# TensorE's expert code as one looped body over 32 half experts, instead of 16 experts written out

## The reference

```
def expert_choice_ffn(h, w_router, w1, w3, w2):
    B, L, D = h.shape
    cap = EC_CAPACITY * L // N_EXPERTS
    aff = jax.nn.softmax((h @ w_router).astype(jnp.float32), axis=-1)
    gate, idx = lax.top_k(aff.transpose(0, 2, 1), cap)
    xs = jax.vmap(lambda hb, ib: hb[ib])(h, idx)
    a = jnp.einsum('becd,edf->becf', xs, w1)
    b = jnp.einsum('becd,edf->becf', xs, w3)
    y = jnp.einsum('becf,efd->becd', jax.nn.silu(a) * b, w2) * gate[..., None].astype(h.dtype)
    return jax.vmap(lambda yb, ib: jnp.zeros((L, D), yb.dtype).at[ib.reshape(-1)].add(yb.reshape(-1, D)))(y, idx)
```

## Time and profile before

| what | us |
|---|---|
| median of three runs | 3301.26 |
| the profiled execution, its own time | 3291.43 |
| its span (first to last instruction) | 3289.7 |
| first expert stage, about 1006 to 1612 | 606 |
| second expert stage, about 2638 to 3236 | 598 |
| TensorE busy in the span | 2851.3 |
| VectorE / ScalarE / GpSimd busy | 867.7 / 492.3 / 238.1 |

### The profile page before, as it was taken

One profiled execution on the slowest core, in us unless ns is written; L12 is line 12 of the kernel. 1 busy time (PEld: TensorE's weight loads), 2 busy tenths in 40 slices (PEclk: granted clock), 3 DMA queues, 4 the chain that ended last, 5 costly groups with the idle time before them and its releaser, 6 DMA issues.

```text
span 3289.7 us, 70042 instructions
## 1 busy us (share of the span) xinstructions
PE 2851.3 (87%) x32580; PEld 2092.8 (64%) x32580; DVE 867.7 (26%) x1443; ACT 492.3 (15%) x862; POOL 238.1 (7%) x254
## 2 busy tenths in 40 slices
PE   6999999999976887887579999999999678878874
PEld 3555676666646787877535456666666378777773
DVE  4953223231142000000159422223311400000003
ACT  2011023331020000000020110333200200000001
POOL 0330000000000000000004100000000000000000
PEclk9999999999988999999889999999999899999997
DMA  7222201102127999999762221121021289999994
GB/s 303 102 109 103 116 29 60 78 26 83 77 81 251 353 349 346 358 349 344 279 236 103 108 99 69 34 79 54 26 109 52 83 306 361 349 348 363 356 340 158
DMA packets 128912, 611.22 MB, mean 186 GB/s; under 512 B 6256, under 2 KB 6256, under 8 KB 119024
## 3 DMA queue, kind: packets, MB, share of 16 engines
q1 hardware_dynamic: 112464, 550.52, 44.1%
q0 software_dynamic: 7168, 24.12, 3.1%
q10 hardware_dynamic: 8992, 32.11, 2.6%
HBM read 576.84 MB, written 29.88 MB: 184 GB/s over the span
## 4 chain that ended last, share of the span: by engine, by line
PE 76%; issue 8%; DVE 8%; DMA 6%; ACT 1%; POOL 0%; POOLq 0%; SPq 0%; DVEq 0%; ACTq 0%
PE ps L281 65%; DVE region_b L1033 4%; DMA ring<-in_w_exp 3%; PE ps L524 2%; DMA ring<-in_w_mix 2%; PE ps L651 1%; PE ps L497 1%; PE ps L507 1%; PE ps L578 1%; PE ps L561 1%; DVE rstd L990 1%; DMA region_x<-ffn_rows 0%; DMA ffn_rows<-region_b,rstd 0%; DVE rstd L982 0%; PE ps L436 0%
## 5 line engine op out<-in xcount | busy, mean ns | idle before, releaser
L281 PE MATMUL ps<-region_r,ring 128*64 128x80 f32 x24192 | 927.6, 237 | 211.7 <-issue 200.3
L281 PEld LDWEIGHTS ps<-region_r,ring 128*64 128x64 f32 x24192 | 892.7, 140 | 248.8 <-issue 237.5
L281 PE MATMUL ps<-hT,ring 128*128 128x320 f32 (+2 forms) x3600 | 1019.2, 441 | 20.7 <-DVE region_b L1021 11.1
L281 PEld LDWEIGHTS ps<-hT,ring 128*128 128x128 f32 x3600 | 610.6, 192 | 380.3 <-issue 237.7
L281 PE MATMUL ps<-region_b,ring 128*128 128x320 f32 (+2 forms) x896 | 257.5, 439 | 3.6 <-DMA ring<-in_w_mix 3.6
L1033 DVE SCALAR_TENSOR_TENSOR region_b<-region_b,params 128x655 f32<-128x655 f32 x240 | 243.8, 1016 | 8.5
L1219 DVE TENSOR_TENSOR region_r<-ps,region_r 128x320 f32<-128x320 f32 x64 | 31.5, 492 | 741.4 <-PE ps L682 741.4
L281 PEld LDWEIGHTS ps<-region_b,ring 128*128 128x128 f32 x896 | 159.3, 191 | 75.8 <-issue 23.3
L954 ACT ACTIVATE region_r<-ps 128x320 f32<-128x320 f32 x64 | 28.0, 438 | 1067.1 <-PE ps L682 1067.1
L281 PE MATMUL ps<-region_x,ring 128*128 128x512 f32 (+1 forms) x480 | 137.7, 445 | 3.7 <-DVE region_x L1159 3.7
L1224 DVE COPY region_r<-ps 128x320 f32<-128x320 f32 x64 | 31.5, 492 | 364.8 <-PE ps L682 364.8
(11 more groups left out here) (193 smaller groups left out, 2009.8 us busy)
## 6 DMA issues: line engine op xcount, KB each, us to landing
ring<-in_w_exp SPq DMA_DIRECT2D x192, 2048.0 KB, 10.7
ring<-in_w_mix SPq DMA_DIRECT2D x68, 2048.0 KB, 11.4
x_store<-region_m ACTq DMA_DIRECT2D x2, 2560.0 KB, 12.1
ffn_rows<-region_r ACTq DMA_DIRECT2D x4, 1280.0 KB, 18.0
region_m<-x_store ACTq DMA_DIRECT2D x2, 2560.0 KB, 10.5
h_rows<-region_x ACTq DMA_DIRECT2D x10, 512.0 KB, 2.7
region_x<-ffn_rows ACTq DMA_DIRECT2D x4, 1280.0 KB, 9.4
rstd<-in_bias POOLq DMA_DIRECT2D x16, 192.0 KB, 2.7
```

The source lines that it names most:

```text
L281: ins = pe.matmul(*args, **kw)
```

## The change

TensorE's work is cut into 32 halves of experts. Half i = 2e + h of expert e has the w1 block and the w3 block of half h of its inner width, and then one w2 block: half h of the outputs of the expert before, e - 1. So each half is three blocks, and the halves look alike. Halves 0 to 2 stand in straight code (the first two without a w2 block), halves 3 to 31 are one body in a loop of TensorE (`pe.Fori(3, HALVES)`), and the two w2 blocks of the last expert follow in straight code. Semaphore values are worked out from the loop's counter in registers.

To make the halves alike, the rest follows: the rows come in halves of 512 columns (34 gathers of 80 x 2 KB, `xs_half`, with row numbers `slot_half` made by VectorE; the last two have no use), each turned between the w1 and the w3 block; VectorE parks them in `xs_next` and copies them to `xs` after the last w3 block of the expert; silu goes into one of two buffers `sil`, since `act` is still read by the w2 blocks; y is handled per half (`turn_y`, `scale_y`, `copy_y`). Products, shapes and weights stay the same. VectorE, ScalarE and GpSimd keep written-out code. The expert weights lie in HBM in the new order (`w_first`, `w_exp`, `w_last`), and SyncE's loop runs over 30 groups of three blocks.

The diff, cut to the parts that move work:

```diff
-                with sp.Fori(0, EPAIRS) as q:
-                    for b in range(2 * EXP_BLOCKS):
-                        s = (MIX_BLOCKS + b) % SLOTS
...
+                for b in range(FIRST_BLOCKS):
+                    expert_load(b, a["w_first"][l, b])
+                with sp.Fori(0, LOOP_BLOCKS // 3) as t:
+                    for b in range(3):
+                        expert_load(FIRST_BLOCKS + b, a["w_exp"][l, t, b], t)
+                for b in range(LAST_BLOCKS):
+                    expert_load(FIRST_BLOCKS + LOOP_BLOCKS + b, a["w_last"][l, b])
...
+                def expert_half(i, n, turns, second, y_before):
+
+                    pe.wait_ge(S["xs_ready"], i + 1 if type(i) is not int or i else 2)
+                    if type(i) is not int or i:
+                        pe.wait_ge(S["sil_ready"], i)
+                    expert_block(n, turns, a_ps, xs, "a_done")
+                    if type(i) is not int or i:
+                        pe.wait_ge(S["xs_parked"], i)
+                    turn_rows(i + 2, i + 3)
+                    if type(i) is not int or i:
+                        pe.wait_ge(S["b_used"], i)
+                    expert_block(n + 1, turns, b_ps, xs, "b_done")
+                    if y_before:
+                        turn_y(i - 3)
+                    if second:
+                        pe.wait_ge(S["act_ready"], i - 1)
+                        expert_block(n + 2, turns, y_ps, act, "y_done")
...
-                turn_rows(0)
-                for q in range(EPAIRS):
-                    expert_pair(q, q == 0, q == EPAIRS - 1)
-                turn_y(NE - 1)
+                turn_rows(0, 2, 0)
+                turn_rows(1, 2, 1)
+                expert_half(0, 0, 0, False, False)
+                expert_half(1, 2, 0, False, False)
+                expert_half(2, FIRST_BLOCKS, 0, True, False)
+                with pe.Fori(3, HALVES) as i:
+                    expert_half(i, FIRST_BLOCKS, i - 2, True, True)
+                for b in range(LAST_BLOCKS):
+                    turn_y(HALVES - 3 + b)
+                    pe.wait_ge(S["act_ready"], HALVES)
+                    expert_block(FIRST_BLOCKS + LOOP_BLOCKS + b, 0, y_ps, act, "y_done")
+                turn_y(HALVES - 1)
...
+                for i in range(HALVES):
+                    sc.wait_ge(S["a_done"], i + 1)
+                    if i >= 2:
+                        sc.wait_ge(S["act_ready"], i // 2 * 2)
+                    sc.activation(sil[i % 2], PS[0][:, 0, 0:HC], ACT.Silu).then_inc(S["sil_ready"], 1)
+                    if i >= 3:
+                        scale_y(i - 3)
...
+                for i in range(HALVES):
+                    e, half = divmod(i, 2)
+                    v.wait_ge(S["rows_turned"], i + 3)
+                    v.tensor_copy(xs_next[:, half * HC:(half + 1) * HC], PS[2][:, 0, 0:HC]).then_inc(S["xs_parked"], 1)
+                    v.wait_ge(S["b_done"], i + 1)
+                    v.wait_ge(S["sil_ready"], i + 1)
+                    if half == 0:
+                        v.tensor_tensor(sil[0], PS[0][:, 1, 0:HC], sil[0], ALU.mult).then_inc(S["b_used"], 1)
+                        if e:
+                            copy_y(i - 2)
+                        continue
                     if e < NE - 1:
-                        take_rows(e + 1)
...
+                        v.wait_ge(S["xs_parked"], i + 1)
+                        v.tensor_copy(flat(xs), xs_next).then_inc(S["xs_ready"], 2)
+                    if e:
+                        copy_y(i - 2)
+                    link(v.tensor_tensor(flat(act)[:, HC:2 * HC], PS[0][:, 1, 0:HC], sil[1], ALU.mult), "b_used")
+                    v.tensor_copy(flat(act)[:, 0:HC], sil[0]).then_inc(S["act_ready"], 2)
...
-                fetch_rows(0)
-                for e in range(NE):
-                    if e + 1 < NE:
-                        fetch_rows(e + 1)
-                    if e:
-                        add_rows(e - 1)
-                add_rows(NE - 1)
+                for n in range(3):
+                    fetch_rows(n)
+                for i in range(HALVES):
+                    if i + 3 < FETCHES:
+                        fetch_rows(i + 3)
+                    if i >= 4 and i % 2 == 0:
+                        add_rows((i - 4) // 2)
+                for e in range(NE - 2, NE):
+                    add_rows(e)
```

More of the change, by code:

```diff
@@ L43 @@
 CAP = CAPL + CAPC
-EPAIRS = NE // 2
+HALVES = 2 * NE
 EPS = 1e-6
@@ L71 @@
 EXP_BLOCKS = 6
+FIRST_BLOCKS, LOOP_BLOCKS, LAST_BLOCKS = 4, 3 * (HALVES - 2), 2
+FETCHES = HALVES + 2
 def tile_count(phase, m):
@@ L191, in step_kernel @@
         ffn_tok = h_tok
-        xs_tok = region_b[0:CAP, 0:D]
+        xs_half = [region_b[0:CAP, b * 512:(b + 1) * 512] for b in range(2)]
         y_tok = region_b[0:CAP, D:2 * D]
@@ L195, in step_kernel @@
         xs = region_r[:, 0:KC * CAP].rearrange("p (k c) -> p k c", k=KC)
+        HC = 4 * CAP
+        sil = [region_r[:, 3200 + b * HC:3200 + (b + 1) * HC] for b in range(2)]
+        xs_next = region_r[:, 3840:3840 + KC * CAP]
         act = region_r[:, 4608:4608 + KC * CAP].rearrange("p (f c) -> p f c", f=KC)
-        yT = region_r[:, 5632:5632 + KC * CAP].rearrange("p (k c) -> p k c", k=KC)
+        yT = region_r[:, 5632:5632 + HC].rearrange("p (k c) -> p k c", k=4)
         logit_row = region_r[:, 2560:3200].rearrange("p (b t) -> p b t", b=2)
@@ L654, in turn, with turn_rows, turn_y, expert_block @@
                     return ins
-                def turn_rows(before):
-                    pe.wait_ge(rows_in, l * (16 * NE) + before * 16 + 16)
-                    for k in range(KC):
-                        last = (pe.transpose if k == KC - 1 else turn)(
-                            x_ps[:, k // 4, (k % 4) * CAP:(k % 4 + 1) * CAP], xs_tok[:, k * P:(k + 1) * P],
-                            ident[0:CAP, 0:CAP])
-                    last.then_inc(S["rows_turned"], 1)
-                def turn_y(before):
-                    pe.wait_ge(S["y_copied"], before * 2 + 2)
-                    if type(before) is not int or before:
-                        pe.wait_ge(S["y_scaled"], before * 2)
-                    for k in range(KC):
-                        last = (pe.transpose if k == KC - 1 else turn)(
-                            yt_ps[0:CAP, k // 4, (k % 4) * P:(k % 4 + 1) * P], yT[:, k, :], ident)
+                def turn_rows(g, fetched, b=0):
+                    pe.wait_ge(rows_in, l * (16 * FETCHES) + fetched * 16)
+                    for k in range(4):
+                        last = (pe.transpose if k == 3 else turn)(
+                            PS[2][:, b, k * CAP:(k + 1) * CAP], xs_half[b][:, k * P:(k + 1) * P], ident[0:CAP, 0:CAP])
+                    last.then_inc(S["rows_turned"], 1)
+                def turn_y(j):
+                    pe.wait_ge(S["y_copied"], j + 1)
+                    pe.wait_ge(S["y_scaled"], j + 1)
+                    for k in range(4):
+                        last = (pe.transpose if k == 3 else turn)(
+                            yt_ps[0:CAP, k * P:(k + 1) * P], yT[:, k, :], ident)
                     last.then_inc(S["y_turned"], 1)
-                def expert_block(q, n, ps, moving, done):
-                    w = weights(l, MIX_BLOCKS + n, q * (2 * EXP_BLOCKS // SLOTS))
+                def expert_block(n, turns, ps, moving, done):
+                    w = weights(l, MIX_BLOCKS + n, turns)
                     for m in range(4):
@@ L1213, in layer_body @@
[L1213 to L1225 removed]
+                flat = lambda t: t.rearrange("p k c -> p (k c)")
@@ L1226, in layer_body @@
+                for j in range(HALVES - 2, HALVES):
+                    copy_y(j)
                 for k in range(KC):
```

112 lines of the change are left out of this document (43 added, 69 removed).

## The result

After the change the median is 3181.5 us (3176.6 to 3183.2, four runs), beside 3298.9 us of the kernel before (3290.5 to 3306.7, four runs): a ratio of 0.9642, with a 95% interval of 0.9615 to 0.9669. That is 117 us off, where 45 were predicted, and it lies outside the range of 3195 to 3320. The profiled execution took 3183.2 us.

What follows compares the result with a forecast made beforehand. The prediction took TensorE's instruction-fetch stalls in the expert stages as the bound, with weight loads next. 2 x (24 from loads - 1.5 around the body) = 45 us off gave 3255 us, range 3195 to 3320.

Steps and rivals of the forecast that it cites:

- What bounds the kernel now: Expert stages: TensorE stalls on instruction fetches, 98.3 us of issue waits in the first; behind them stand the weight loads.
- The body stays: TensorE's half-expert loop body, near 800 records, stays in instruction memory; 87 of 96 blocks per layer lose their stall.
- Rival 1: TensorE's loop body doesn't stay and is fetched anew after each branch: -40 to +465 us, about 3505 us; chance 0.15.
- The sum of the loads: Weight loads of an expert stage: idle time, fetch packets, gathers and rate together take 24 us off per layer.
- The rate at full share: Expert-stage loads with DMA engines fully busy: 363 GB/s taken, where rows gave 360, so 5 us off per layer.
- rival 3: Expert stages: two loads always in the queue bring the rate near 406 GB/s; about 3200 us, chance 0.11.
- 5% of 606 us is idle time of the DMA engines: Expert stage: 30 us idle, some 7 us at the start and 5 us at the end; 18 us can be filled.
- Packets and gathers: Expert stage: fewer fetch packets save 5.8 us; 34 half-row gathers cost 0 to +21 us, taken as +5.
- The lower end of the range: 3195 us: 406 GB/s on all weights, 201 MB in 496 us plus 42 of gathers, 54 us off per layer.
- A new wait: Half-row gathers inside an expert stage might land late for TensorE; judged hidden with 5 us to spare.
- Around the body: Start and end of each expert stage: an extra gather issue and half-index operations cost +1.5 us per layer.
- the stretches outside stay within 3 us: Sign to check: program stretches outside the two expert stages change by no more than 3 us.

Runs made afterwards that it cites:

- written-out version: The changed kernel with halves 3 to 31 written out in TensorE's program instead of looped; 3297.8 us, ratio 0.9996.
- aligned loop: The kernel before with experts 2 to 14 as one looped TensorE body, its head at the start of a 16 KB piece; 3190.0 us, ratio 0.9679.
- unaligned expert loop: The kernel before with experts 2 to 14 as one looped TensorE body, its head not placed at a piece's start; 3358.3 us, ratio 1.0197.

## Why the prediction was wrong

**What bounds the kernel now: right.** TensorE's instruction fetches were the stall. The written-out version keeps all else and keeps the stall (78.3 us in 400) and the time.

**The body stays: right.** 86 packets (about 90 forecast), 13 in the first stage (10 to 15), issue 6.3 us (under 20), the wait for loads 54.8 us at the seams (50 to 80). The second stage has 50.5 us in 67 waits for loads and 9.5 us for issue. Rival 1 is refuted for this body and shown for a larger one. The argument from GpSimd's and SyncE's packets pointed the right way; the size was left open, and the aligned loop fits 128 KB.

**The sum of the loads: the step that failed.** "The rate at full share: 360 by the rows, at most the 406 GB/s of the opening stretch ... I take 363, near the row of the same stage: -5 us." Over the stage it was 378 at a share of 1.00, and 381 inside. Before, the first stage moved 606 us x 341 GB/s = 206.6 MB. At 359 GB/s that is 576 us, at 378 it is 547: the term is 29 us, not 5. The reason is not a faster engine but a wrong reading: I took the rate divided by the share in a disturbed stretch as a property of the DMA engines. The run with 10 extra products shows that late slots alone bring it down to the 359 of before. A load that starts on idle engines starts slowly (the run with one load at a time), and this counts as busy. The stretch of before that I held against rival 3, 359 GB/s at 1014 to 1041 us, misled too. The changed kernel has, there, in the 27 us behind it, and from 1066 us to the end of its loop:

```profile
1014.00:1041.00 27.00, 23.55 (x640) 22.66 (x637) 3.09 (x7) 0.88 (x2) 1.91 (x3) 1.00 1.01 374
1041.00:1068.00 27.00, 22.12 (x584) 21.13 (x585) 2.60 (x6) 1.12 (x2) 0.91 (x1) 1.00 0.98 360
1066.00:1539.00 473.00, 418.60 (x10987) 397.21 (x10984) 50.13 (x113) 32.06 (x57) 45.01 (x41) 1.00 1.03 391
```

374/1.01 = 370 and 360/0.98 = 367 against 391/1.03 = 380. The first two stretches are straight code and the first pass of the loop, which still fetch: ten of the 13 fetch packets of the stage start between 1007 and 1065 us, none in the third stretch. So the row stood for a piece with fetches, in both kernels, and not for the inside. That the fetches are the whole difference is not shown: from 1066 to 1118 us, behind the last of them, the changed kernel still moves only 372 GB/s at a share of 1.01.

**"5% of 606 us is idle time of the DMA engines ... 18 us can be filled":** the share over the whole stage reached 1.00, so the 7 us of the start and 5 us of the end that I held back were made up for too: 30 us. The start and the end still have idle engines (144 and 139 GB/s in the first and last fortieth of the stage), but inside the stage the share passes 1.

**Packets and gathers:** the first stage now moves 544 x 378 = 205.6 MB, 1.0 MB less, 3 us, where 5.8 - 5 = 1 us was forecast. The gathers' "0 to +21 us" are about zero on their queue: 6.9% of 606 us and 7.7% of 544 us are both 42 us of the engines. 30 + 29 + 3 = 62 us, as measured, and it must be so, since share, rate and bytes multiply to the time; forecast were 18 + 5 + 1 = 24. The lower end of the range had 496 us of weights, 42 us of gathers and 12 us of idle ends, 550 in all. The queues of the stage took 498 us for the weights (91.6% of 544, for 195 MB within it, not 201) and 42 us for the gathers; what did not come are the 12 us.

**A new wait: rightly discarded.** No gather was waited for beyond the first two.

**Around the body:** "the stretches outside stay within 3 us" failed in the profiled execution: between the stages it is 7.7 us longer. Of the +1.5 us for the first gathers, little came: from TensorE's turns just ahead of them (2630.19 and 2575.55 us) to the first product of the second stage it takes 7.5 us before and 7.8 us after. Some 5 us are lost in the second layer's input projections, whose code did not change. That work there, before:

```profile
1790.00:1905.00 115.00, 108.76 (x383) 59.07 (x382) 63.34 (x71) 20.60 (x35) 31.62 (x27) 0.99 0.29 114
```

and after:

```profile
1729.00:1849.00 120.00, 112.56 (x384) 60.66 (x383) 63.02 (x71) 20.66 (x35) 31.33 (x26) 0.94 0.28 110
```

TensorE has the same work there with a granted clock of 0.99 and 0.94: the lower clock stands where the time is lost. It does not go with the change. The changed kernel with 16 KB pieces, and the unaligned expert loop, which is the kernel before with stalls in its stage, have there:

```profile
1720.00:1835.00 115.00, 109.33 (x385) 59.48 (x384) 63.76 (x72) 20.95 (x36) 31.70 (x27) 0.99 0.29 114
1805.00:1925.00 120.00, 112.72 (x383) 60.85 (x382) 63.09 (x72) 20.82 (x35) 31.26 (x26) 0.94 0.28 110
```

From the last product of one stage to the first of the next it takes 1027.7 us before, 1035.0 after, 1028.1 in the changed kernel with 16 KB pieces and 1033.7 in the unaligned loop. Each of these is one execution, so the 7.7 us are no cost of the change that these runs show.

**Rival 3 ("full rate", 3200 us, chance 0.11)** was nearest. It named the cause, two loads always in the queue, and got 378 of its 406 GB/s. The 406 belonged to an opening whose loads come in packets of 16 KB; with these, the changed kernel moves 402 GB/s from 1100 to 1500 us. Its chance was too small because the rows held against it came from stretches with fetches and slots that come back late.

## What to carry to other kernels

When a long straight program stalls an engine inside its blocks on "issue", try a loop. Here it was worth 62 us in the first stage: more than the 30 us of idle time that the DMA engines showed, but less than the 98 us of the stall, since the loads became the bound. Count the body's records, keep it with the piece ahead within eight 16 KB pieces on TensorE, and set its head on a piece's start. Do not take the rate per busy share of a stretch in which consumers return buffers late as what the transfers can do; the slow starts are hidden in the share. Keep single 16 KB packets away from loads that spread over 16 engines, or split them.

## What the runs showed of the hardware

- A loop body of TensorE over seven pieces of 16 KB stays (110 packets, 3190 us); the same body with its head elsewhere is fetched anew after 13 of 24 branches (227 packets, 3358 us). This fits a memory of eight pieces. A branch whose target is gone costs 6.5 us (at a DMA share of 0.85, and 6.6 us at 0.33), 2.4 us more after two products, and 2.3 us by a granted clock of 0.63 after the idle time.
- One 16 KB packet on one engine beside 2 MB loads: 96 per layer cost 170 us, 32 cost 55 us, the bytes of 96 in 1 KB rows 18 us.
- Late slots lower the rate per busy share from 381 to 359 GB/s, with packets over 300 ns going from 0.06% to 3.24%, 88% of them in the first 2.5 us after a load is issued.
- Matmuls of 64 columns of weights that all go to the same columns, each with a sum of its own, took 73 ns each, and 39 ns in the same run in the kernel's alternation of two column halves. Which of the two differences does it was not tried.
